# Two weight arrays begin 128 bytes later in SBUF, at multiples of 256 instead of odd multiples of 128

## The chip, the cores and the metric

The program runs on one core of a Trainium2 chip (8 cores, two dies). The metric is the device time in microseconds of one execution, the median of several. Lower is better. Five engines matter: TensorE (PE in the profile, with its weight loads as PEld), VectorE (DVE), ScalarE (ACT), GpSimd (POOL) and SyncE (SP), which issues the transfers of the weights.

## What is computed

Two kinds of transformer layer, two of each, run one after the other on one sequence of 512 tokens of width 1024 in float32. Cut to what matters here:

```python
for l in range(DEPTH):                       # DEPTH = 2, first kind
    h = rms_norm(x, norm_mix[l])
    z = h @ w_in[l]                          # then attention, a gated recurrence, a convolution
    x = x + mix @ w_out[l]
    h = rms_norm(x, norm_mlp[l])
    x = x + jnp.square(jax.nn.relu(h @ w_mlp_in[l])) @ w_mlp_out[l]
for l in range(DEPTH):                       # second kind: four mixers, gates, w_branch, w_out
    ...
    x = x + jnp.square(jax.nn.relu(h2 @ w_ff1)) @ w_ff2
```

Most of the work is in the products with weights: `w_in`, `w_out`, `w_branch` and the two matrices of each MLP.

## The kernel before

Everything is kept transposed in SBUF: 128 partitions hold features, 512 columns hold tokens. The weights come from memory as 518 units of 128 x 1024 float32 (512 KB), in the fixed order of the list `UNITS`; a layer of the first kind has 92 of them and one of the second kind 167. Each unit goes through the same steps:

- SP loads it into one of the two buffers of `w_raw` (`load_unit`, L255), as soon as the unit two before it has been split.
- ACT copies it to one of the three buffers of `w_hi` as fp32r, a float32 cut to the digits that one pass of TensorE takes (`split_hi`, L231), as soon as PE has finished the unit three before it.
- POOL computes the rest, `w_raw - w_hi`, into the same buffer of `w_lo` (`split_lo`, L278). For 36 units of the first two layers DVE does it (`split_lo_dve`, L247).
- PE multiplies: for each of 8 blocks of the inner dimension three matmuls add into one bank, high by high (L334), low weight by high activation (L335) and high weight by low activation (L336), in `Group.part`; `Group.some` has the same three at L306 to L308. The weight block is the stationary operand (128 x 128, 512 bytes of a partition), the activation the moving one (128 x 512). So the three matmuls of a block need three weight loads, from `w_hi`, `w_lo` and `w_hi`, and the whole program has 518 x 8 x 3 = 12,432 such pairs of load and matmul.

The activations are split in the same way by DVE: `hH` and `hL` for the input of a layer, `H2` and `L2` for that of an MLP, `midH` and `midL` for its hidden part. The other matmuls (attention, recurrence, sums) are plain float32 and don't touch the weight arrays.

The four engines work on the units in a ring, tied by semaphores; the order on each engine is written out by hand. DVE, ACT and POOL work beside PE. DVE's other work stands between the stages: norms (`pair`, L406), decays and gaps of the recurrences (L858, L2120), softmax (L749), the mixing of the branches (L2060).

SBUF is laid out by a stack: each call of `sb` puts a tensor behind the last one and fills it up to a multiple of `ALIGN` = 128 bytes. Four constants of 32 bytes each and a scratch of 2,048 bytes stand first, so the first tensor of the program, `xT`, begins at byte 2,176 of a partition, an odd multiple of 128. The sizes that follow are multiples of 256 up to the small tensors behind `yt`, except for `masks`; so `hH`, `hL`, `w_raw`, `w_hi`, `w_lo` and the constants `C` begin at odd multiples of 128 too, and `pair` and `yt` at multiples of 256. Of the tensors of the stages, those at multiples of 256 are, in the first two layers, `terms`, `probs`, `probsT`, `gap`, `QK` and a few more of the recurrence, and in the last two the compression weights `cw`. The others, `midH`, `midL`, `H2`, `L2`, `Z` and in the last two layers the counterparts of `probs`, `probsT`, `gap` and `QK` among them, are at odd multiples of 128. (The profile writes the counterparts under the same names, since it leaves numbers out.)

Of the kernel before, what the change touches and what calls it, by code (L numbers as in the profile page):

```python
# [19 lines left out]
U8 = mybir.dt.uint8  # L20
# [4 lines left out]
P = 128  # L25
# [16 lines left out]
ALIGN = 128  # L42
# [61 lines left out]
def program(nc, given, out):  # L104
# [5 lines left out]
    with ctx:  # L110
        used = {}

        def sb(name, shape, dt=F32, scope=ctx):


            used[name] = used.get(name, 0) + 1
            name = f"{name}_{used[name]}"
            tile = scope.enter_context(nc.sbuf_tensor(name, shape, dt))
            rest = (-(int(np.prod(shape[1:])) * BYTES[dt]) // 32 * 32) % ALIGN
            if rest:  # L120
                scope.enter_context(nc.sbuf_tensor(f"{name}_pad", [P, rest], U8))
            return tile
# [11 lines left out]
        hL = sb("hL", [P, NK, T], F32R)  # L134
        rstd = sb("rstd", [P, T])
        w_raw = sb("w_raw", [P, 2, UNIT])
        w_hi = sb("w_hi", [P, WB, UNIT], F32R)
        w_lo = sb("w_lo", [P, WB, UNIT], F32R)
        C = sb("C", [P, len(CONSTS), P])
        ident, ones, pair_ones, rot1, rot2, neg_tri, neg_ones = (C[:, i, :] for i in range(7))  # L140
        later_one = C[:, 10, :]
        Cb = sb("Cb", [P, 4, P], BF16)
# [107 lines left out]
        def load_unit(u):  # L250
            layer, j, _, nk, ntile, _ = UNITS[u]
            w = nk * ntile * P
            if u >= 2:
                wait_lo(sp, u - 2)
            sp.dma_start(w_raw[:, u % 2, 0:w], (w1_in if layer < DEPTH else w2_in)[layer % DEPTH, j, :, 0:w])\  # L255
                .then_inc(w_loaded[u % 2], 16)

        def load_vec(layer):
            n = NV1 if layer < DEPTH else NV2
            sp.dma_start(vecs[layer % 2][:, 0:n], (vec1_in if layer < DEPTH else vec2_in)[layer % DEPTH])\  # L260
                .then_inc(vec_loaded, 16)
# [701 lines left out]
        def load_start():  # L963

            scope = ExitStack()
            with scope:
# [4 lines left out]
                def on_sync():  # L971
                    sp.dma_start(C[:, 0, :], consts_in[:, 0, :]).then_inc(consts_loaded, 16)
                    load_vec(0)
                    load_unit(0)
                    for half in range(2):
                        c = slice(half * D // 2, half * D // 2 + D // 2)
                        sp.dma_start(x_tok[:, :, c], x_in[0, :, c].rearrange("(t p) d -> p t d", p=P))\
                            .then_inc(x_loaded[half], 16)
                    load_unit(1)
                    sp.dma_start(C[:, 1:, :], consts_in[:, 1:, :]).then_inc(matrices_loaded, 16)  # L980
                    sp.dma_start(masks_f[:, :, :], masks_in).then_inc(masks_loaded, 16)
                    sp.dma_start(pos[:, :], pos_in[0:1, :].to_broadcast([P, T])).then_inc(pos_loaded, 16)
                    sp.dma_start(freq[:, :], freq_in).then_inc(pos_loaded, 16)
                    sp.dma_start(cosT[:, :], rope_in[0]).then_inc(rope_loaded, 16)
                    sp.dma_start(sinT[:, :], rope_in[1]).then_inc(rope_loaded, 16)
# [26 lines left out]
                def on_vector():  # L1012
# [7 lines left out]
                    dve.wait_ge(matrices_loaded, 16)  # L1020
                    dve.tensor_copy(Cb[:, 0, :], C[:, 0, :])
                    dve.tensor_copy(Cb[:, 1:4, :], C[:, 7:10, :])
                    dve.wait_ge(pos_loaded, 32)
# [1289 lines left out]
```

## Time and profile before

| | |
|---|---|
| median of 3 runs | 3797.75 us (3796.26 to 3799.45) |
| profiled execution | 3801.36 us |
| its span, first to last instruction | 3800.0 us |
| mean granted TensorE clock | 0.977 |
| PE busy | 3653.7 us, 96% of the span |
| PEld busy | 2813.1 us, 74% |
| DVE busy | 2157.0 us, 57% |
| ACT busy | 1309.1 us, 34% |
| POOL busy | 1197.5 us, 32% |

The busy time of an engine counts each moment once, however many of its instructions overlap in it. Matmuls are pipelined: one begins before the last has ended, so the distance from one start to the next, and not the duration, is what a matmul costs in a dense stretch.

### The profile page before, as it was taken

The numbers are of one execution on the slowest core, as the hardware profiler recorded it, in microseconds if no ns is written. First come the engines' busy times: TensorE is split into PE (matmuls) and PEld (weight loads), VectorE is DVE, ScalarE is ACT, GpSimd is POOL, SyncE is SP. The second block draws the span as 40 slices with busy tenths as digits, with TensorE's granted clock in tenths as the row PEclk, the third lists the DMA queues.
The fourth block names the chain that finished last, engine by engine and source line by source line (L and its number), as shares of the span: only waits on it lengthen the run. The fifth ranks groups of instructions, "written<-read, shape, count | busy, mean of one in ns | idle before, by whom it ended". The sixth has DMA issues, their size and how long they took to land.

```text
span 3800.0 us, 44699 instructions
## 1 busy us (share of the span) xinstructions
PE 3653.7 (96%) x17876; PEld 2813.1 (74%) x17876; DVE 2157.0 (57%) x3048; ACT 1309.1 (34%) x2226; POOL 1197.5 (32%) x486
## 2 busy tenths in 40 slices
PE   8889999998899999999999999999999999999998
PEld 6646888865588888676777678887767777778887
DVE  7787565688754474633374485545553255365444
ACT  6344121443522131545423531122354433342112
POOL 0002444200144443132333244444213232334443
PEclk9889999997999999999999999999999999999999
DMA  4101333220033333121222132334112122223332
GB/s 134 44 12 50 98 97 95 93 69 12 23 95 99 95 120 105 40 67 56 78 62 77 51 93 96 95 99 147 51 34 79 61 78 62 67 73 95 97 97 83
DMA packets 80797, 292.38 MB, mean 77 GB/s; under 512 B 9648, under 2 KB 11088, under 8 KB 80080
## 3 DMA queue, kind: packets, MB, share of 16 engines
q1 hardware_dynamic: 77808, 278.49, 23.5%
q10 hardware_dynamic: 2784, 11.03, 0.9%
q8 instruction: 143, 2.34, 0.2%
q14 instruction: 62, 0.51, 0.0%
HBM read 285.30 MB, written 2.10 MB: 76 GB/s over the span
## 4 chain that ended last, share of the span: by engine, by line
PE 85%; DVE 11%; issue 2%; ACT 2%; DMA 0%; SPq 0%; DVEq 0%; ACTq 0%
PE acc L334 23%; PE acc L336 22%; PE acc L335 22%; PE banks L939 2%; PE banks L658 2%; PE banks L614 2%; DVE conv_c L1317 2%; PE banks L641 2%; PE banks L950 1%; DVE stat L738 1%; PE banks L1648 1%; DVE probs L749 1%; DVE QK L867 1%; DVE w_lo L247 1%; DVE pair L406 1%
## 5 line engine op out<-in xcount | busy, mean ns | idle before, releaser
L278 POOL TENSOR_TENSOR w_lo<-w_raw,w_hi 128x1024 fp32r<-128x1024 f32 x482 | 1197.3, 2484 | 2575.5 <-ACT w_hi L231 2575.5
L231 ACT ACTIVATE w_hi<-w_raw 128x1024 fp32r<-128x1024 f32 x518 | 548.9, 1060 | 1725.2 <-PE acc L336 1641.7
L334 PE MATMUL acc<-hH,w_hi 128*128 128x512 f32 x1776 | 732.3, 412 | 13.2 <-DVE sig L2036 6.6
L336 PE MATMUL acc<-hL,w_hi 128*128 128x512 f32 x1776 | 700.6, 395 | 0.0
L335 PE MATMUL acc<-hH,w_lo 128*128 128x512 f32 x1776 | 699.6, 394 | 0.0
L334 PEld LDWEIGHTS acc<-hH,w_hi 128*128 128x128 f32 x1776 | 338.5, 191 | 99.2 <-issue 25.0
L334 PE MATMUL acc<-H,w_hi 128*128 128x512 f32 x1024 | 400.5, 391 | 3.8 <-DVE L L398 3.8
L369 DVE TENSOR_TENSOR xT<-acc,xT 128x512 f32<-128x512 f32 x160 | 110.6, 691 | 517.0 <-PE acc L336 498.5
L334 PE MATMUL acc<-midH,w_hi 128*128 128x512 f32 x1024 | 401.0, 392 | 0.3
L335 PE MATMUL acc<-midH,w_lo 128*128 128x512 f32 x1024 | 398.8, 389 | 0.0
L336 PE MATMUL acc<-midL,w_hi 128*128 128x512 f32 x1024 | 398.7, 389 | 0.0
L336 PE MATMUL acc<-L,w_hi 128*128 128x512 f32 x1024 | 398.5, 389 | 0.0
L335 PE MATMUL acc<-H,w_lo 128*128 128x512 f32 x1024 | 398.5, 389 | 0.0
L336 PEld LDWEIGHTS acc<-hL,w_hi 128*128 128x128 f32 x1776 | 337.5, 190 | 73.7
L335 PEld LDWEIGHTS acc<-hH,w_lo 128*128 128x128 f32 x1776 | 338.9, 191 | 66.7 <-issue 4.3
L334 PEld LDWEIGHTS acc<-midH,w_hi 128*128 128x128 f32 x1024 | 192.2, 188 | 46.3 <-DVE midL L506 7.0
L334 PEld LDWEIGHTS acc<-H,w_hi 128*128 128x128 f32 x1024 | 192.2, 188 | 45.9 <-DVE L L398 5.5
L335 PEld LDWEIGHTS acc<-H,w_lo 128*128 128x128 f32 x1024 | 192.2, 188 | 40.6 <-issue 1.0
L336 PEld LDWEIGHTS acc<-midL,w_hi 128*128 128x128 f32 x1024 | 192.2, 188 | 40.2
L336 PEld LDWEIGHTS acc<-L,w_hi 128*128 128x128 f32 x1024 | 192.2, 188 | 40.0
L335 PEld LDWEIGHTS acc<-midH,w_lo 128*128 128x128 f32 x1024 | 192.3, 188 | 39.3
L505 DVE CAST midH<-relu 128x512 fp32r<-128x512 f32 x64 | 160.2, 2504 | 2.2
(332 smaller groups left out, 4716.7 us busy)
## 6 DMA issues: line engine op xcount, KB each, us to landing
w_raw<-in_stream SPq DMA_DIRECT2D x518, 512.0 KB, 3.6
cw<-in_cmpw ACTq DMA_DIRECT2D x2, 2048.0 KB, 7.3
mixed<-in_cmpw ACTq DMA_DIRECT2D x2, 2048.0 KB, 12.6
x_tok<-in_x SPq DMA_DIRECT2D x2, 1024.0 KB, 7.4
out<-probsT SPq DMA_DIRECT2D x4, 512.0 KB, 4.0
stack<-Z ACTq DMA_DIRECT2D x8, 128.0 KB, 2.2
stack<-Z ACTq DMA_DIRECT2D x8, 127.8 KB, 2.4
masks_f<-in_masks SPq DMA_DIRECT2D x1, 960.0 KB, 11.9
```

The costliest lines, as they stand in the source:

```text
L231: act.activation(w_hi[:, u % WB, 0:w], w_raw[:, u % 2, 0:w], ACT.Copy).then_inc(hi_split, 1)
L278: pool.tensor_tensor(w_lo[:, u % WB, 0:w], w_raw[:, u % 2, 0:w], w_hi[:, u % WB, 0:w], ALU.subtract)\
L334: pe.matmul(acc[n % 2][:, :], wh, H[:, k, :], start=(k == 0), stop=False)
L335: pe.matmul(acc[n % 2][:, :], wl, H[:, k, :], start=False, stop=False)
L336: last = pe.matmul(acc[n % 2][:, :], wh, Lo[:, k, :], start=False, stop=(k == nk - 1))
L369: dve.tensor_tensor(xT[:, i, :], a[:, :], xT[:, i, :], ALU.add).then_inc(up(free), 1)
L505: link(dve, dve.tensor_copy(midH[:, i, :], r))
L614: last = pe.matmul(self.score_banks[h % 3][:, 0:m], w["q"][r, qt * P:(qt + 1) * P], w["k"][r, lo * P:hi * P], start=True, stop=True, skip_ ...
L641: last = pe.transpose(self.turn_banks[n % 2][:, j * P:(j + 1) * P], self.P[:, s % 3, a, j * P:(j + 1) * P], ident)
L658: pe.matmul(self.out_bank[HD * a:HD * a + HD, cols], w["v"](kt, a), self.PT[:, a, kt, cols], start=(first and kt == 0), stop=True, skip_gr ...
L939: last = pe.matmul(scores, KK[r, jt * P:(jt + 1) * P], moving, start=(j == 0), stop=True, skip_group_check=True)
L1317: ins = dve.scalar_tensor_tensor(conv_c[:, j, :], src, vec[:, w:w + 1], conv_c[:, j, :], ALU.mult, ALU.add)
```

## The change

Two unused tensors of 128 bytes are put into the stack, one ahead of `w_hi` and one behind `w_lo`:

```diff
         w_raw = sb("w_raw", [P, 2, UNIT])
+        sb("ahead_of_halves", [P, ALIGN], U8)
         w_hi = sb("w_hi", [P, WB, UNIT], F32R)
         w_lo = sb("w_lo", [P, WB, UNIT], F32R)
+        sb("behind_halves", [P, ALIGN], U8)
         C = sb("C", [P, len(CONSTS), P])
```

Nobody writes or reads them. The addresses in a partition, from the two built programs:

| tensor | before | remainder by 256 | after | remainder by 256 |
|---|---|---|---|---|
| `w_raw` | 53,376 | 128 | 53,376 | 128 |
| `w_hi` | 61,568 | 128 | 61,696 | 0 |
| `w_lo` | 73,856 | 128 | 73,984 | 0 |
| `C` | 86,144 | 128 | 86,400 | 128 |
| all behind `C` | | | 256 higher | as before |

`xT`, `hH`, `hL` and `rstd` stand ahead of the arrays and don't move. Every engine issues the same instructions in the same order with the same semaphores; only addresses differ, and the line numbers behind the edit are two higher.

## Rows read from the trace of the kernel before

**Rows 1.** The page: busy time of each engine; then the clock in 40 slices.

```profile
PE 3653.7 (96%) x17876; PEld 2813.1 (74%) x17876; DVE 2157.0 (57%) x3048; ACT 1309.1 (34%) x2226; POOL 1197.5 (32%) x486
...
PEclk9889999997999999999999999999999999999999
```

**Rows 2.** Busy us by window in two MLPs: PE, PEld, DVE, ACT, POOL, clock.

```profile
540.00:640.00 100.00, 99.99 (x442) 82.48 (x441) 48.99 (x48) 20.17 (x19) 44.22 (x19) 1.00 0.32 99
2400.00:2500.00 100.00, 99.99 (x441) 82.49 (x440) 43.96 (x43) 19.94 (x19) 44.58 (x19) 1.00 0.32 97
```

**Rows 3.** The page, groups: count | busy us, mean ns | idle before.

```profile
L278 POOL TENSOR_TENSOR w_lo<-w_raw,w_hi 128x1024 fp32r<-128x1024 f32 x482 | 1197.3, 2484 | 2575.5 <-ACT w_hi L231 2575.5
L231 ACT ACTIVATE w_hi<-w_raw 128x1024 fp32r<-128x1024 f32 x518 | 548.9, 1060 | 1725.2 <-PE acc L336 1641.7
L334 PEld LDWEIGHTS acc<-hH,w_hi 128*128 128x128 f32 x1776 | 338.5, 191 | 99.2 <-issue 25.0
```

**Rows 4.** Timeline of an MLP of the first layer: start us, duration us.

```profile
620.04 0.39 PE L335 MATMUL acc<-midH,w_lo 128*128 128x512 f32 x1
...
622.11 1.06 ACT L231 ACTIVATE w_hi<-w_raw 128x1024 fp32r<-128x1024 f32 x1 [4.38 <-PE acc L336]
...
623.25 2.40 POOL L278 TENSOR_TENSOR w_lo<-w_raw,w_hi 128x1024 fp32r<-128x1024 f32 x1 [3.04 <-ACT w_hi L231]
...
625.48 0.39 PE L335 MATMUL acc<-midH,w_lo 128*128 128x512 f32 x1
```

**Rows 5.** Weight loads of L1648: duration ns min/median/max, first and last start.

```profile
L1648 PEld LDWEIGHTS banks<-cblocks,cw x128: 186/192/193, 1481.4 to 2676.6; 128*128 128x128 f32 x128
L1648 PEld LDWEIGHTS banks<-cblocks,mixed x128: 191/192/193, 1500.3 to 2695.5; 128*128 128x128 f32 x128
```

**Rows 6.** Timeline of L1648, PE alone: sixteen matmuls with each weight tensor.

```profile
1481.78 1.95 PE L1648 MATMUL banks<-cblocks,cw 128*128 128x62 f32 x16
...
1500.80 1.95 PE L1648 MATMUL banks<-cblocks,mixed 128*128 128x62 f32 x16
```

**Rows 7.** Line L641, first two layers and then the last two.

```profile
L641 PEld LDWEIGHTS banks<-C,probs x256: 137/141/232, 246.2 to 1005.0; 128*128 128x128 f32 x128
...
L641 PEld LDWEIGHTS banks<-C,probs x464: 137/140/146, 1538.0 to 3360.6; 128*128 128x128 f32 x155
```

**Rows 8.** Float32 matmuls with moving operand `pair`, and with `soft_sb`.

```profile
L413 PE MATMUL banks<-pair,C x16: 590/592/593, 27.7 to 3439.8; 128*128 128x512 f32 x16
...
L1722 PE MATMUL banks<-soft_sb,C x32: 589/592/697, 1721.4 to 3008.2; 128*128 128x512 f32 x32
```

**Rows 9.** Two groups of ACT by form.

```profile
L957 ACT ACTIVATE sp_part_sb<-sp_part_sb 128x512 f32<-128x512 f32 x32 | 20.2, 631 | 1.0
...
L957 ACT ACTIVATE terms<-terms 128x512 f32<-128x512 f32 x16 | 10.1, 633 | 0.5
```

**Rows 10.** Line L867 of DVE, first two layers and then the last two.

```profile
L867 DVE TENSOR_TENSOR QK<-Z,gap x72: 674/684/2254, 98.6 to 910.7; 128x512 f32<-128x512 f32 x72
...
L867 DVE TENSOR_TENSOR QK<-Z,gap x36: 677/684/694, 1913.8 to 3179.0; 128x512 f32<-128x512 f32 x36
```

**Rows 11.** Line L278, POOL's subtraction: durations.

```profile
L278 POOL TENSOR_TENSOR w_lo<-w_raw,w_hi x482: 2342/2404/2971, 6.6 to 3770.8; 128x1024 fp32r<-128x1024 f32 x161
```

**Rows 12.** Waits of PEld: who waited for POOL, us in total, times, longest.

```profile
PEld acc L334 <- POOL w_lo L278: 1.8, 3, 0.8
```

**Rows 13.** Timeline of a stage between the MLPs: POOL and DVE.

```profile
1898.76 2.39 POOL L278 TENSOR_TENSOR w_lo<-w_raw,w_hi 128x1024 fp32r<-128x1024 f32 x1 [4.29 <-ACT w_hi L231]
1898.83 3.41 DVE L2120 TENSOR_TENSOR_SCAN cum<-C,Z 128x512 f32<-128x512 f32 x1
```

**Rows 14.** Chain that ended last: start us, us, piece.

```profile
153.62 2.75 DVE Z L1364
...
1906.98 1.23 DVE cum L2120
...
3434.56 2.89 DVE pair L406
```

## The prediction

> **What bounds the kernel now.** I read the page first. PE is busy 96% of the span and its clock stands near full speed in nearly all slices [rows 1]; the other engines are busy 57% of the span at most. Then two windows of 100 us in the MLPs of the first and of the third layer: PE is never free there, at granted clock 1.00, and 442 and 441 matmuls touch each window, which is one every 227 ns [rows 2]. The timeline gives it more exactly: from a matmul of L335 that starts at 620.04 to one that starts at 625.48 there are 24 matmuls, 5.44 / 24 = 226.7 ns apart [rows 4]. Each of them has a weight load of its own; the load lasts 188 to 191 ns, but lies under the matmul before it [rows 3]. The 12,432 pairs at 226.7 ns make 2818 us, 74% of the span. So the time is PE's pace in this stream, and behind it the stages between the MLPs, where PE and DVE take turns on the chain [rows 14].
>
> Durations come from the profiled execution, 3801.36 us, with a span of 3800.0 us. The median of the runs is 3797.75 us, 3.6 us or 0.1% less, so differences are carried over to the median one for one.
>
> **What the change does, part by part.** It adds no instruction, wait or transfer, and moves none. The two new tensors are never touched. What is left are the instructions that read or write `w_hi` and `w_lo` at their new place. Everything behind the arrays keeps its remainder by 256, and `w_raw`, into which the transfers go, doesn't move at all, so no transfer of weights gets another start. What could differ for the tensors behind is only a remainder by 512 or more. `midH` is at remainder 384 by 512 in the first layer and at 128 in the third, and the two windows show the same pace [rows 2]: 0 for that.
>
> Term 1, the weight load. If loads from a multiple of 256 were quicker or slower, it would show where PE does little but load. Line L1648 is such a place: 62 columns move through each 128 x 128 block of weights. Its weights come once from `cw`, at a multiple of 256, and once from `mixed`, at an odd multiple of 128, with the same moving operand. The loads have the same median, 192 ns [rows 5], and sixteen matmuls take 1.95 us with either [rows 6]. Line L641 agrees: it loads `probs` from a multiple of 256 in the first two layers and from an odd multiple of 128 in the last two, at medians of 141 and 140 ns [rows 7], while its moving operand in `C` is at an odd multiple of 128 in both. So the case that the change makes, weights at a multiple of 256 against a moving operand at an odd multiple of 128, is in the trace already and costs nothing there. Likewise a moving operand at a multiple of 256 (`pair`) and at an odd multiple of 128 (`soft_sb`) against weights in `C` take 592 ns both [rows 8]. Cost: 0 x 12,432.
>
> The Trainium skill says of this (page "SBUF — State Buffer", section "SBUF: two separate sides" with its table of ports) that TensorE reads the moving operand and the weights through two ports of their own that wait for nobody; by that rule the place of the weights could not matter, and the rows above agree.
>
> What no row shows is the same pair of places in fp32r with 512 columns, since all such matmuls use the two arrays. I bound it. From below: 512 columns at 2.4 GHz are 213.3 ns, so at most 226.7 - 213.3 = 13.4 ns can go, 12,432 x 13.4 = 167 us. From above I take as much again, since the trace shows no collision to price: the load of 191 ns [rows 3] has 36 ns of room in 226.7. I take 0, the value of the nearest rows. Between lie steps of one tick of 2.4 GHz, 0.42 ns, or 5.2 us over the stream.
>
> Term 2, ACT's copy into `w_hi`, 1060 ns [rows 3]. ACT writes 512 elements in 631 ns at an odd multiple of 128 and in 633 ns at a multiple of 256 [rows 9], 2 ns apart. It is hidden too: in the MLP the copy ends at 623.17, POOL's subtraction at 625.65 [rows 4], and PE needs the unit only after two others, 2 x 5.44 us after it released the buffer near 622.1, at about 633. Cover 7 us; 0.
>
> Term 3, POOL's subtraction, which reads `w_hi` and writes `w_lo`: 482 times, median 2404 ns [rows 11]. Nearly nobody waits for its result, 1.8 us in all [rows 12], and POOL sits idle 2575.5 us [rows 3]. It costs time in another way. At 1898.83 DVE starts a scan and holds it for 3.41 us, over POOL's subtraction from 1898.76 to 1901.15, [rows 13], though the same scan of the next run takes 1.23 us on the chain [rows 14]. Going through the whole chain I find 31 pieces of DVE of more than 2 us of this kind, from 153.62 to 3434.56, of which the first and the last are shown [rows 14]. So each nanosecond of the subtraction may cost up to 31 ns of the chain. The trace has no subtraction on POOL at another place. DVE's product of two SBUF operands, L867, has a median of 684 ns with both `gap` and `QK` at multiples of 256 and with both at odd multiples of 128 [rows 10], and is the nearest row by kind. The ends are POOL's own spread [rows 11]: 62 ns less than the median gives 31 x 0.062 = 1.9 us, 567 ns more gives 31 x 0.567 = 17.6 us. I take 0.
>
> Term 4, DVE's 36 subtractions L247 on the same arrays: by the same row of L867, 0.
>
> Sum: 0 + 0 + 0 + 0, so 3797.75, rounded to 3798 us. A measurement of this kernel tells about 0.2% from no change, 7.6 us.
>
> **The rivals.** A, the stream gets faster (0.07). The 13.4 ns over the 213.3 could be the meeting of the two reads, since the weights and the moving operands now start at the same remainder by 256. If all of it went, the time would be 3798 - 167 = 3631 us; two ticks of 0.42 ns give 3788. Against it: rows 5 to 8 show no sign of the remainder.
>
> The Trainium skill (page "TensorE: Matmul & The Clock Gate", section "Wait — 56ns, not 53.3ns?") gives 215.7 ns from start to start for warm bf16 matmuls of 512 columns; this trace has 226.7 ns, and if placement explained the 11 ns between them, 12,432 x 11 = 137 us would go, an estimate of 3661 us. The page names no placement.
>
> B, slower by POOL (0.03). One mechanism: the subtraction takes longer at the new place, and each of the 31 DVE pieces on the chain that waits for it to end grows with it. At 10% (240 ns) it is 7.4 us, 3805 us, the point from which it decides; at 20%, 14.9 us and 3813 us. It needs no delay of PE by `w_lo` itself. C, slower by PE (0.03): the new remainder makes a meeting of reads where there was none. Two ticks give 10.4 us, 3808 us; the 13.4 ns of the upper bound give 3965 us. D, POOL gets 10% quicker (0.01): 3790 us.
>
> The change not doing what it says is no rival: the addresses are in the program, and the arrays are at their new places.
>
> **How the numbers follow.** The forecast of no effect has 0.86. Faster is A and D, 0.08; slower is B and C, 0.06. Within the forecast the median may move by what the three runs show, 3796.26 to 3799.45, some 1.6 us to each side, and by small changes in how DVE and POOL meet on the chain, which I allow 3 us more. With a tick of PE's pace to each side (5.2 us), which also takes in the lower end of POOL's bound, the range is 3791 to 3805 us. What lies outside is the body of the rivals, under 0.14.
>
> **What would show it.** In the profile after, the line of L278 keeps its median near 2404 ns, the weight loads of the stream theirs of 188 to 191 ns, ACT's copy 1060 ns, and 24 matmuls of the MLP take 5.44 us; the chain still has some 31 long pieces of DVE. A step of the pace would show as other than 441 or 442 matmuls in a window of 100 us: at 213.3 ns it would be 469. If POOL is the cause, the median of L278 moves and `pair` at L406 on the chain with it (2.89 us now). The prediction is wrong if fp32r streams care for a remainder that float32 matmuls don't care for, or if POOL does where DVE doesn't.

## The result, and the profile after

| | us | runs | range |
|---|---|---|---|
| before | 3798.18 | 4 | 3796.26 to 3799.45 |
| after | 3861.44 | 4 | 3859.35 to 3861.95 |

The ratio of the runs is 1.0163, with a 95% interval of 1.0151 to 1.0175. The kernel is slower by 63 us, and above the predicted range of 3791 to 3805 us. The profiled execution after took 3861.95 us, with a span of 3860.6 us, 60.6 us longer than before.

The page after, its first lines and its clock, as in [rows 1]:

```profile
span 3860.6 us, 44699 instructions
...
PE 3720.3 (96%) x17876; PEld 2818.8 (73%) x17876; DVE 2152.9 (56%) x3048; ACT 1309.6 (34%) x2226; POOL 1202.1 (31%) x486
...
PEclk9889999997999999999999999999999999999999
```

PE is still busy 96% of the time, so no new idle time has come in, and the clock is as it was. The same two windows in the MLPs as in [rows 2]. The columns are the stretch, its length, then busy time with the number of instructions for PE, PEld, DVE, ACT and POOL, PE's granted clock, DMA share and GB/s:

```profile
540.00:640.00 100.00, 100.00 (x431) 80.59 (x430) 43.62 (x42) 19.10 (x18) 43.85 (x18) 1.00 0.32 95
2400.00:2500.00 100.00, 100.00 (x431) 80.86 (x430) 50.87 (x48) 19.10 (x18) 43.48 (x18) 1.00 0.32 95
```

431 matmuls touch each window, where 442 and 441 did. The granted clock is 1.00 (the level of 2.4 GHz) in both, so the clock is not the reason. The timeline of PE at the place of [rows 4]: start us, us, instruction. L337 is the L335 of before.

```profile
620.10 0.39 PE L337 MATMUL acc<-midH,w_lo 128*128 128x512 f32 x1
...
625.70 0.39 PE L337 MATMUL acc<-midH,w_lo 128*128 128x512 f32 x1
```

24 matmuls lie between the two rows, 5.60 / 24 = 233.3 ns apart, where it was 226.7. The other lines that the prediction named, from the page's groups and from the answers on POOL's line, the waits and the chain:

```profile
L280 POOL TENSOR_TENSOR w_lo<-w_raw,w_hi 128x1024 fp32r<-128x1024 f32 x482 | 1201.9, 2494 | 2630.9 <-ACT w_hi L233 2630.9
L233 ACT ACTIVATE w_hi<-w_raw 128x1024 fp32r<-128x1024 f32 x518 | 548.7, 1060 | 1781.8 <-PE acc L338 1702.9
...
L336 PEld LDWEIGHTS acc<-hH,w_hi 128*128 128x128 f32 x1776 | 339.7, 191 | 104.8 <-issue 24.6
...
L280 POOL TENSOR_TENSOR w_lo<-w_raw,w_hi x482: 2340/2410/2973, 6.8 to 3830.8; 128x1024 fp32r<-128x1024 f32 x161
...
PEld acc L336 <- POOL w_lo L280: 1.5, 2, 0.8
...
3486.74 2.89 DVE pair L408
```

ACT's copy takes 1060 ns as before, the load shows 191 ns as before, POOL's subtraction a median of 2410 ns against 2404, and PEld waits 1.5 us for POOL, where it waited 1.8 [rows 3, 11, 12]. The last long piece of `pair` on the chain has the same 2.89 us as in [rows 14].

**Where the 60.6 us are.** I took from both traces the distance from the start of each matmul of the stream to the start of the next. Distances of 260 ns or more, which are pauses, count with the rest of the span. Worked out so:

| | distances | sum us | mean ns | rest of the span us |
|---|---|---|---|---|
| before | 11,723 | 2664.5 | 227.3 | 1135.5 |
| after | 11,710 | 2724.7 | 232.7 | 1135.9 |

The stream takes 60.2 us more and everything else 0.4 us more. After, 13 distances fewer (about 3 us) count with the stream and stand with the rest; all 12,432 matmuls of the stream have a record in both traces. That doesn't change the reading: the loss is PE's pace. It is even: with hH, midH, H2 and yH as the moving operand, in the first two layers and in the last two, the means are 232.6 to 232.9 ns. It does not depend on who else is at work: while POOL is busy the mean is 232.7 ns and while it is idle 232.7; for ACT it is 232.6 and 232.7, for DVE 232.6 and 232.8. Before, the distances in the stream are 226 and 227 ns one after the other. After, they go up and down between 228 and 241 ns in patterns that repeat, near 540 us for instance 230, 232, 228, 230, 233, 241, 232.

### The profile page after: what moved, and what is told of

It reads as the page before. It is cut to its first block, busy times and chain, and to the rows that moved or that the text cites. A ratio compares the mean times of both kernels' runs of the same rounds, so it can differ in the third digit from the quotient of the medians.

```text
span 3860.6 us, 44699 instructions
## 1 busy us (share of the span) xinstructions
PE 3720.3 (96%) x17876; PEld 2818.8 (73%) x17876; DVE 2152.9 (56%) x3048; ACT 1309.6 (34%) x2226; POOL 1202.1 (31%) x486
## 4 chain that ended last, share of the span: by engine, by line
PE 85%; DVE 11%; issue 2%; ACT 2%; DMA 0%; SPq 0%; DVEq 0%; ACTq 0%
PE acc L336 23%; PE acc L338 23%; PE acc L337 23%; PE banks L941 3%; PE banks L660 2%; PE banks L616 2%; DVE conv_c L1319 2%; PE banks L643 2%; PE banks L952 1%; DVE stat L740 1%; PE banks L1650 1%; DVE probs L751 1%; DVE QK L869 1%; DVE w_lo L249 1%; DVE pair L408 1%
## 5 line engine op out<-in xcount | busy, mean ns | idle before, releaser
L233 ACT ACTIVATE w_hi<-w_raw 128x1024 fp32r<-128x1024 f32 x518 | 548.7, 1060 | 1781.8 <-PE acc L338 1702.9
L336 PE MATMUL acc<-hH,w_hi 128*128 128x512 f32 x1776 | 740.9, 417 | 11.9 <-DVE sig L2038 6.2
L338 PE MATMUL acc<-hL,w_hi 128*128 128x512 f32 x1776 | 708.6, 399 | 0.0
L337 PE MATMUL acc<-hH,w_lo 128*128 128x512 f32 x1776 | 708.2, 399 | 0.0
L336 PEld LDWEIGHTS acc<-hH,w_hi 128*128 128x128 f32 x1776 | 339.7, 191 | 104.8 <-issue 24.6
L336 PE MATMUL acc<-H,w_hi 128*128 128x512 f32 x1024 | 406.2, 397 | 3.3 <-DVE L L400 3.3
L336 PE MATMUL acc<-midH,w_hi 128*128 128x512 f32 x1024 | 406.3, 397 | 0.0
L337 PE MATMUL acc<-H,w_lo 128*128 128x512 f32 x1024 | 404.2, 395 | 0.0
L337 PE MATMUL acc<-midH,w_lo 128*128 128x512 f32 x1024 | 404.1, 395 | 0.0
L337 PEld LDWEIGHTS acc<-hH,w_lo 128*128 128x128 f32 x1776 | 340.5, 192 | 73.3 <-issue 4.3
L336 PEld LDWEIGHTS acc<-H,w_hi 128*128 128x128 f32 x1024 | 192.7, 188 | 51.3 <-DVE L L400 5.0
L336 PEld LDWEIGHTS acc<-midH,w_hi 128*128 128x128 f32 x1024 | 192.7, 188 | 49.6 <-DVE midL L508 5.2
L337 PEld LDWEIGHTS acc<-H,w_lo 128*128 128x128 f32 x1024 | 192.7, 188 | 46.3 <-issue 1.0
L337 PEld LDWEIGHTS acc<-midH,w_lo 128*128 128x128 f32 x1024 | 192.7, 188 | 44.6
L507 DVE CAST midH<-relu_sb 128x512 fp32r<-128x512 f32 x64 | 160.6, 2509 | 2.2
```

Source lines behind the costliest of these rows:

```text
L233: act.activation(w_hi[:, u % WB, 0:w], w_raw[:, u % 2, 0:w], ACT.Copy).then_inc(hi_split, 1)
L336: pe.matmul(acc[n % 2][:, :], wh, H[:, k, :], start=(k == 0), stop=False)
L337: pe.matmul(acc[n % 2][:, :], wl, H[:, k, :], start=False, stop=False)
L338: last = pe.matmul(acc[n % 2][:, :], wh, Lo[:, k, :], start=False, stop=(k == nk - 1))
L507: link(dve, dve.tensor_copy(midH[:, i, :], r))
```

## The experiments

The theory that I formed: what counts is the place of the weights against the place of the moving operand, modulo 256 bytes. Before, both start at an odd multiple of 128, a difference of 0; after, the difference is 128. The rivals: the place of the weights by itself (loads from multiples of 256 are slow); the space between the tensors, and what moved by 128 between the two gaps; and contention with ACT and POOL, which write the two arrays. Below, "difference" is the start of the moving operand less that of the weights, modulo 256. The mean distances in the stream (pauses left out as above) come from the trace of each run. The three lines of the stream, L334 to L336 before, stand some lines lower in the kernels with more lines, up to L346.

**1. Weights or gap.** Four kernels; the edits are gaps that nothing touches.

```diff
+ sb("gap_0", [P, 256], U8)    # e1: ahead of w_hi
+ sb("gap_0", [P, 128], U8)    # e2: ahead of w_hi
+ sb("gap_1", [P, 128], U8)    # e2: ahead of w_lo
+ sb("gap_0", [P, 128], U8)    # e3: ahead of w_lo
+ sb("gap_1", [P, 128], U8)    # e3: ahead of C
+ sb("gap_0", [P, 128], U8)    # e4: ahead of xT, the first tensor
```

> Both weight arrays 256 bytes later, so they begin at odd multiples of 128 again, and everything behind them 256 bytes later, just as in the changed kernel. In the trace of the changed kernel a matmul of the stream starts every 232.7 ns instead of 226.8. Theory 1 (the remainder of the weights by 256 against that of the moving operand) and theory 2 (the remainder of the weights by itself): pace 226.8 ns, time 3798 us. Theory 3 (what costs is that the tensors behind the arrays have moved by 256, or the distance between w_raw and the arrays): pace near 232.7 ns, about 3861 us.

> Only w_hi at a multiple of 256, w_lo at an odd multiple of 128. w_hi is loaded for two of the three matmuls of a block. If each load pays for its own place (theories 1 and 2): 2/3 of the 63 us, 3840 us, with the pace lost only where w_hi is loaded. If what counts is that w_hi and w_lo are alike (theory 4: successive loads from different remainders): as slow as or slower than 3861 us or, if unlike is good, below 3798 us.

> Only w_lo at a multiple of 256. Theories 1 and 2: one load of three pays, 3798 + 21 = 3819 us, and e2 and e3 together make the 63 us. Theory 4 (alike or unlike) gives the same time for e2 and e3.

> 128 bytes ahead of xT: weights, hH, hL, H2, L2, midH, midL all begin at multiples of 256, their remainders relative to one another are those of the kernel before. Theory 1 (relative): pace 226.8 ns, 3798 us. Theory 2 (the weights' own remainder): pace 232.7 ns, about 3861 us.

| | moved by 128 | time us | ratio, 95% interval | mean ns after hi x H, lo x H, hi x L, in the MLPs |
|---|---|---|---|---|
| e1 | nothing (256) | 3797.84 | 0.9998, 0.9988 to 1.0007 | 226.8 to 226.9 |
| e2 | `w_hi` alone | 3864.73 | 1.0173, 1.0157 to 1.0188 | 232.8, 234.8, 232.2 |
| e3 | `w_lo` alone | 3838.47 | 1.0109, 1.0092 to 1.0126 | 232.5, 234.1, 226.7 |
| e4 | everything | 3799.59 | 1.0001, 0.9992 to 1.0010 | 226.7 to 226.9 |

The windows of e1, e3 and e4, columns as above:

```profile
2400.00:2500.00 100.00, 99.98 (x441) 82.47 (x440) 43.57 (x42) 19.52 (x19) 45.00 (x19) 1.00 0.31 96
```

```profile
2400.00:2500.00 100.00, 100.00 (x433) 81.36 (x432) 46.21 (x44) 19.11 (x18) 43.63 (x19) 1.00 0.31 95
```

```profile
2400.00:2500.00 100.00, 99.99 (x442) 82.46 (x441) 43.63 (x43) 19.11 (x19) 43.72 (x18) 1.00 0.31 98
```

441 matmuls in e1 and 442 in e4, as before, 433 in e3. e2 and e3 did not come out as expected (3840 and 3819 us): they lose 65 and 39 us beside the runs of before that were taken with them, 104 together and not 63. So it is not that each load pays a price of its own, which adds up. e1 moves the weights, and all that lies behind them, by 256, and loses nothing: neither the gap nor the remainder by 512 matters. e4 puts the weights at multiples of 256, exactly as the change does, but the activations too, and loses nothing: the place of the weights by itself does not matter either. What is left is the difference between the two.

**2. The activations instead of the weights.** e8 leaves the remainder of the weights by 256 as it was and moves all high and low activations by 128. The two gaps around `hH` and `hL` stand ahead of the weights and move `w_raw`, `w_hi` and `w_lo` by 256 bytes, which e1 showed to cost nothing.

```diff
  xT = sb("xT", [P, NK, T])
+ gap_of(128)
  hH = sb("hH", [P, NK, T], F32R)
  hL = sb("hL", [P, NK, T], F32R)
+ gap_of(128)
...  # the same around midH and L2, midH2 and midL2, yH and yL, H2_2 and L2_2
```

> All activations of the stream at multiples of 256, weights where they were before. Theory 1 (relative): the same difference of 128 as in the changed kernel, 3861 us and 232.7 ns. Theory 2: 3798 us and 226.8 ns.

It took 3865.36 us, ratio 1.0172 (1.0156 to 1.0187), with means of 232.3 to 232.7 ns. The window of e8:

```profile
2400.00:2500.00 100.00, 100.00 (x431) 80.90 (x430) 50.85 (x49) 19.10 (x18) 43.46 (x19) 1.00 0.31 95
```

431 matmuls, as after the change, although `w_raw`, `w_hi` and `w_lo`, all that ACT and POOL read and write for the weights, have kept their remainder by 256. With e4 this settles the cause as far as places go: it is relative.

**3. Half of the activations.** In e6 only the low halves are moved, in e7 only the high ones. The gaps are those of e8, around each low or each high array.

```diff
+ gap_of(128)    # e6: ahead of hL and behind it; e7: ahead of hH and behind it
...  # the same around the halves of mid, H2, y and H2_2
```

> Only the low halves of the activations (hL, L2, midL, yL) at multiples of 256; they move through PE in the third matmul of a block, L336. Theory 1a: a weight load is held up by the matmul that it lies under, when the two read from different remainders; then one load of three is held, the distance after the third matmul and the one after the first of the next block grow to 232 to 234 ns and the one after the second stays 227; time like e3_lo_only, 3838 us. Theory 1b: a matmul is slow when its own weights and its moving operand differ; then the distances after the second and the third matmul grow and the one after the first stays 227; also near 3838 us. Theory 2: 3798 us.

> Only the high halves of the activations (hH, H2, midH, yH) at multiples of 256, which move in the first two matmuls of a block. Theories 1a and 1b: two loads or matmuls of three differ, like e2_hi_only, 3865 us. Theory 2 (the weights' own remainder): 3798 us.

e6 took 3856.23 us, ratio 1.0152 (1.0137 to 1.0168); e7 took 3821.50 us, ratio 1.0059 (1.0042 to 1.0075). Expected were 3838 and 3865 us, so this is the wrong way round for a simple count. In e6 one matmul in three (hi x L) has a difference of 128, in e7 two in three (hi x H and lo x H). Yet in the last two layers with `H2` e6 shows 230.0, 235.8 and 234.2 ns, 20 ns more per three matmuls than 3 x 226.7, and e7 228.4, 232.5 and 225.9 ns, 7 ns more. In the first two layers e6 shows 227.0, 229.0 and 234.3 there. The numbers of the first two layers are means over two paces. The timeline of e6 in one MLP, around a short pause, with `midH` and `midL`:

```profile
591.36 0.39 PE L340 MATMUL acc<-midH,w_hi 128*128 128x512 f32 x1
...
593.42 0.39 PE L340 MATMUL acc<-midH,w_hi 128*128 128x512 f32 x1
...
595.93 0.40 PE L342 MATMUL acc<-midL,w_hi 128*128 128x512 f32 x1
596.30 0.50 PE L340 MATMUL acc<-midH,w_hi 128*128 128x512 f32 x1
596.64 0.39 PE L341 MATMUL acc<-midH,w_lo 128*128 128x512 f32 x1
...
597.10 0.39 PE L340 MATMUL acc<-midH,w_hi 128*128 128x512 f32 x1
...
599.20 0.39 PE L340 MATMUL acc<-midH,w_hi 128*128 128x512 f32 x1
```

Ahead of the pause nine matmuls in 2.06 us are 228.9 ns each, behind it nine in 2.10 us are 233.3 ns. `H2` of the same layer has the quick pace from 377 to 414 us, over more than six units and so over all three buffers of the weights, and the slow one from 636 to 680 us. The same tensors at the same places thus have two paces, each of which repeats (226, 227, 234 ns, and 230, 236, 234 ns after hi x H, lo x H and hi x L) until a pause. In the MLPs of the last two layers nearly all blocks have the slow one. The price is not a fixed sum for each matmul.

**4. Which read meets which.** While PE streams the columns of one matmul, PEld loads the weights of the next. The expectations call one form of the theory 1a: the load meets the moving operand of the matmul that it lies under. The other is 1b: what counts is a matmul's moving operand against its own weights. e12 tells them apart. Its order is hi x H, hi x L, lo x H, with `w_lo` and the low activations at multiples of 256. Then every load lies under a matmul with the same remainder, but two matmuls of three differ from their own weights. e13 has the new order alone.

```diff
  pe.matmul(acc[n % 2][:, :], wh, H[:, k, :], start=(k == 0), stop=False)
- pe.matmul(acc[n % 2][:, :], wl, H[:, k, :], start=False, stop=False)
- last = pe.matmul(acc[n % 2][:, :], wh, Lo[:, k, :], start=False, stop=(k == nk - 1))
+ pe.matmul(acc[n % 2][:, :], wh, Lo[:, k, :], start=False, stop=False)
+ last = pe.matmul(acc[n % 2][:, :], wl, H[:, k, :], start=False, stop=(k == nk - 1))
...
+ gap_of(128)    # e12: ahead of w_lo and behind it, and around each low activation
```

> The second and third matmul of a block exchanged: high by high, high weight by low activation, low weight by high activation. All arrays at odd multiples of 128 as before. All theories: 226.8 ns and 3798 us; it is the base for e12.

> The same order, with w_lo and the low halves of the activations at multiples of 256 and the high halves at odd multiples of 128. Now each weight load lies under a stream that begins at the load's own remainder (high weights under high activation, low weights under low activation, high weights under high activation), while two of three matmuls have weights and moving operand at different remainders. Theory 1a (a load is held up by the stream that it lies under): 226.8 ns and 3798 us, no loss at all. Theory 1b (a matmul's own two operands): two of three matmuls slow, 231 to 233 ns, 3840 to 3865 us.

e13 took 3799.21 us, ratio 0.9998 (0.9988 to 1.0009). e12 took 3839.34 us, ratio 1.0107 (1.0090 to 1.0124), with a mean distance of 231.2 ns. The window of e12:

```profile
2400.00:2500.00 100.00, 100.00 (x432) 80.73 (x431) 46.06 (x44) 19.11 (x18) 43.79 (x19) 1.00 0.32 95
```

432 matmuls. So 1a falls as the whole cause: no load has another remainder than the operand it lies under, and 39 us are lost. 1b fits in size (two thirds of 63 us would be 42), but even the distance after hi x H, where the matmul's own operands are alike too, has grown, to 230.9 ns in the MLPs, and it does not fit the others: two of three differ in e7 and in e2 too, and 23 and 65 us are lost; one of three differs in e3 and in e6, and 39 and 57 us are lost. In e3 the distance after hi x H has grown too (232.5 ns), whose own operands are alike but under which `w_lo` is loaded from another remainder. Neither form holds alone.

**5. Other differences.** In e5 and e11 each pair of activations has a difference of its own, so that one run shows several. In e11 all activations but `hH` and `hL`, which have a gap, are slices that begin 1 to 60 elements inside a larger tensor.

```diff
+ gap_of(64)     # e5: ahead of hH; 192 behind hL; others ahead of and behind mid, H2, y
...
+ def sb_at(name, n, off, scope=ctx):    # e11
+     t = sb(name, [P, n * T + 64], F32R, scope)
+     return t[:, off:off + n * T].rearrange("p (k t) -> p k t", t=T)
```

> Weights stay at odd multiples of 128; the activations move by amounts that differ by stage. Activation minus weights by 256: hH and hL 64, midH and midL 192 in the first two layers and 224 in the last two, H2 and L2 32 and 96, yH and yL 128. If only the remainder by 128 of the difference counts in the sense of two banks of 128 bytes, 32 to 96 (partly in the other bank) lie between 226.7 and 232.7 ns and 128 is the worst; if every difference but 0 is as bad, all stages are near 232.7. yH at 128 is the control: weights where they were and activation moved, 232.7 ns by theory 1, 226.8 by theory 2 (weights' own remainder). The whole time is read only beside that.

> Activation minus weights by 256, by stage: hH and hL 160; H2 and L2 16 in the first two layers and 8 in the last two; midH and midL 4 and 240; yH and yL 48. e5_map had 229 ns at 64 and 232.5 to 233.4 ns at 32, 96, 128, 192 and 224. If the loss comes as soon as the two differ at all, every stage here is at 229 to 234 ns; if it needs a difference of some tens of bytes, 4, 8 and 16 stay at 226.8 ns. A stage below 226.7 ns would show a place that is better than that of the kernel before.

e5 took 3848.79 us, ratio 1.0131 (1.0110 to 1.0151), and e11 3876.86 us in its one run, beside 3798.04 us for the kernel before. The mean distances, with those of the runs above:

| difference, bytes | mean ns | run and operand |
|---|---|---|
| 0 | 226.7 | before, e4 |
| 4 | 236.6 | e11, mid, first layers |
| 8 | 233.4 | e11, H2, last layers |
| 16 | 231.7 | e11, H2, first layers |
| 32 | 233.3 | e5, H2, first layers |
| 48 | 232.0 | e11, y |
| 64 | 229.3 | e5, hH |
| 96 | 233.4 | e5, H2, last layers |
| 128 | 232.5 to 232.9 | after; e5, y |
| 160 | 234.1 | e11, hH |
| 192 | 233.3 | e5, mid, first layers |
| 224 | 233.3 | e5, mid, last layers |
| 240 | 235.4 | e11, mid, last layers |

The timeline of e11 in `midH` (difference 4):

```profile
619.87 0.40 PE L346 MATMUL acc<-midL,w_hi 128*128 128x512 f32 x1
...
625.55 0.40 PE L346 MATMUL acc<-midL,w_hi 128*128 128x512 f32 x1
```

and of e5 in `hH` (difference 64):

```profile
760.00 0.39 PE L342 MATMUL acc<-hL,w_hi 128*128 128x512 f32 x1
...
765.50 0.39 PE L342 MATMUL acc<-hL,w_hi 128*128 128x512 f32 x1
```

24 matmuls lie between each pair of rows: 5.68 / 24 = 236.7 ns and 5.50 / 24 = 229.2 ns. Of thirteen differences 0 is the best, 64 the next, and one of 4 bytes is the worst. It is no matter of even and odd multiples of 128 alone. The order of the others is weaker: most stand for one stage of one run, the stages have slightly different means at difference 0 too (226.7 ns for H2, 226.9 for mid, 227.9 for hH, 227.2 for y), and e6 has shown paces 4.4 ns apart at one and the same difference.

**6. Why the rows of before said nothing.** The prediction argued from matmuls of 62 and 128 columns. e9 and e10 take 512, 256, 128 and 384 columns in the MLPs and projections of layers 1 to 4, so the other columns of the tokens are left out of the computation; e10 also has the gaps of the change.

```diff
+ COLS = (512, 256, 128, 384)
...
+ m = COLS[UNITS[u][0]]
...
- pe.matmul(acc[n % 2][:, :], wh, H[:, k, :], start=(k == 0), stop=False)
+ pe.matmul(acc[n % 2][:, 0:m], wh, H[:, k, 0:m], start=(k == 0), stop=False)
...
+ gap_of(128)    # e10: ahead of w_hi, and behind w_lo
```

> The kernel before with shorter streams: 512 columns of the activation move in the first layer as before, 256 in the second, 128 in the third, 384 in the fourth, so 3/4 to 1/4 of the tokens are left out of the products from the second layer on. Weights and activations at the same remainder by 256. Shows the pace by columns: 226.7 ns at 512 and, if the extra over the columns (13.4 ns at 2.4 GHz) is a cost of each matmul, about 173 at 384 and 120 at 256; at 128 the load binds, near the 112 ns of L1648.

> The same shorter streams with the weight arrays at multiples of 256, as in the changed kernel. Theory 1 with a fixed cost for each load: 6 ns more than e9_cols_same at 512, 384 and 256. With a cost for each column: 6, 4.5 and 3 ns. At 128 columns, where the load binds: no difference, as the rows of L1648 and L641 had none, which would show why these rows misled; a difference of 6 ns there would mean that float32 and fp32r behave differently.

e9 took 3451.65 us and e10 3479.65 us, in one run each. Their mean granted clock was 0.846 and 0.845, where the kernel before has 0.977, and it was 0.50 (the level of 1.2 GHz) in the MLP of the third layer of both. The windows there, with 128 columns, first of e9 and then of e10:

```profile
2100.00:2140.00 40.00, 39.74 (x187) 39.56 (x187) 19.71 (x19) 7.42 (x7) 19.14 (x8) 0.50 0.33 95
```

```profile
2100.00:2140.00 40.00, 40.00 (x187) 39.48 (x186) 34.82 (x31) 9.57 (x10) 19.57 (x8) 0.50 0.29 92
```

187 matmuls in either, one every 213 ns, so with 128 columns there is no loss at that level either. The mean distances at granted clock 1.00:

| columns | e9, difference 0 | e10, difference 128 |
|---|---|---|
| 512 | 227.0 | 232.5 |
| 384 | 173.7 | 175.8 |
| 256 | 119.7 | 118.9 |
| 128 | 111.7 | 111.7 |

The timelines of e9 with 384, 256 and 128 columns:

```profile
2434.99 0.33 PE L341 MATMUL acc<-hH,w_hi 128*128 128x384 f32 x1
...
2439.15 0.33 PE L341 MATMUL acc<-hH,w_hi 128*128 128x384 f32 x1
...
1223.65 0.28 PE L343 MATMUL acc<-midL,w_hi 128*128 128x256 f32 x1
...
1229.40 0.28 PE L343 MATMUL acc<-midL,w_hi 128*128 128x256 f32 x1
...
1543.52 0.27 PE L342 MATMUL acc<-hH,w_lo 128*128 128x128 f32 x1
...
1548.89 0.27 PE L342 MATMUL acc<-hH,w_lo 128*128 128x128 f32 x1
```

and those of e10:

```profile
2660.99 0.34 PE L343 MATMUL acc<-hH,w_hi 128*128 128x384 f32 x1
...
2665.21 0.34 PE L343 MATMUL acc<-hH,w_hi 128*128 128x384 f32 x1
...
1227.47 0.28 PE L345 MATMUL acc<-midL,w_hi 128*128 128x256 f32 x1
...
1233.17 0.28 PE L345 MATMUL acc<-midL,w_hi 128*128 128x256 f32 x1
...
1563.94 0.28 PE L344 MATMUL acc<-hH,w_lo 128*128 128x128 f32 x1
...
1569.30 0.28 PE L344 MATMUL acc<-hH,w_lo 128*128 128x128 f32 x1
```

With 384 columns 24 matmuls lie between the rows, 4.16 / 24 = 173.3 ns against 4.22 / 24 = 175.8. With 256 and with 128 there are 48: 5.75 / 48 = 119.8 against 5.70 / 48 = 118.8, and 5.37 / 48 = 111.9 against 5.36 / 48 = 111.7. The other remainder costs 5.5 ns with 512 columns, 2.1 with 384 and nothing with 256 or 128. A row of matmuls with 62 or 128 columns could not have shown it.

## Why the prediction was wrong, point by point

**Term 1 failed, and it alone.** The step was: "So the case that the change makes, weights at a multiple of 256 against a moving operand at an odd multiple of 128, is in the trace already and costs nothing there", and from it "Cost: 0 x 12,432". The rows were read rightly, and they have not changed: after, the loads of L1648 and L641 of before still have medians of 192 and 140 ns. But they carry 62 and 128 columns, and e10 shows that a difference of 128 is free in the stream too when the matmuls are that short. At 512 columns the term measures 232.7 - 227.3 = 5.4 ns; times the 11,710 distances that is 63 us, less 3 us for the 13 distances fewer (13 x 227 ns): the 60.2 us of the accounting. The lines of `C` [rows 8] do have 512 columns, but they are float32, and slower: the 592 ns are durations, and two in a row take 0.86 us on the chain after the change, 430 ns each, nearly twice what a matmul of the stream takes.

```profile
3491.72 0.86 PE banks L415 x2
```

I did not measure whether the meeting is hidden there or does not exist for float32.

The text named this weak place itself ("What no row shows is the same pair of places in fp32r with 512 columns") and put it down to "fp32r streams". e9 and e10 show the length to matter, within fp32r. Whether fp32r matters besides stays open. The term's bound from above, 13.4 ns, did hold the 5.4 ns, but the chance that it was given, 0.03 for rival C, was far too small: with the bound at 167 us and no row of the same kind, the nearest rows deserved less trust.

**The rule on the ports.** With 512 columns every run with a difference other than 0 shows PE's pace to depend on where its two operands lie against each other: 226.7 ns at 0, up to 236.6 at 4 bytes. The Trainium skill (page "SBUF — State Buffer", section "SBUF: two separate sides") was read in the prediction as saying that the place of the weights cannot matter. By that reading e8, after and e11 would all have kept 226.7 ns; the measurement decides, and the reading falls for matmuls of 384 and 512 columns. At 256 and 128 columns no run speaks against it; only the difference 128 was tried there.

**Rival C was the case** as far as shown: PE slower by the new remainder. That the reads meet, as it says ("the new remainder makes a meeting of reads where there was none"), is argued. It was sized at two ticks, 3808 us, and at most at 3965; the mean was 5.4 ns or 13 ticks, 3861 us. Rival A, that the reads met before and would be freed, had the sign wrong: 0 is the one difference without a loss. As for the 13.4 ns above the columns' own time, they remain at 512, 384 and 256 columns with difference 0: 226.7 - 213.3 = 13.4, 173.3 - 160.0 = 13.3, 119.8 - 106.7 = 13.1 (the columns at 2.4 GHz). So they don't grow with the columns, as the loss by the difference does. What they are is not shown.

**Terms 2, 3 and 4 and the tensors behind held.** ACT 1060 ns and 1060; POOL 2404 and 2410 ns, which by the 31 pieces would be 0.2 us; the long DVE pieces of the chain are the same in number and sum (33 of over 1.3 us in each trace, 87.1 and 87.2 us). Rivals B and D therefore did not occur. The tensors behind cost nothing, as e1 shows.

**What the prediction's signs told.** It asked for 24 matmuls in 5.44 us, and for 441 or 442 per window. Both showed the fault at once: 5.60 us and 431. The loads' 188 to 191 ns did not: the load shows 191 ns still.

**What stays open.** Shown is that the loss is in the stream's pace, that it follows the difference of the places modulo 256, and that at a difference of 128 it is there with 384 and 512 columns and not with 256. Not shown is which read holds up which, or that a meeting of reads is the cause at all. 1a alone is refuted by e12. 1b does not add up between e6, e7 and e12. The repeating patterns, and the two paces of e6 for the same instructions, suggest that the phase between a load and the stream settles into one of several steady forms. That is argued, not shown, and the records of the loads don't show it: in both paces of e6 a load starts 2 to 4 ns behind the start of a matmul and takes 187 or 188 ns. Pauses differ from kernel to kernel, so such kernels can't be sized better than some ns per matmul from the map above.

## What to carry to other kernels

In a dense stream of fp32r matmuls of 512 columns, give the weights and the moving operands starts that are equal modulo 256 bytes, all of them, high and low halves alike, and check it after each edit that allocates something ahead of one of them: it is worth 5.4 ns in 227 per matmul here, and up to 10. When a price is looked up in other rows of a trace, take rows that are bound by the same thing. A matmul bound by its weight load says nothing of one that is bound by its columns. Take the same length too: with 256 columns, where the columns also set the pace, the difference cost nothing (118.9 against 119.7 ns).

## What the runs showed of the hardware

- A shift of 4 bytes between the operands costs more (236.6 ns, one run) than one of 128 (232.7 ns) or of 64 (229.3 ns).
- The pace of load and matmul in fp32r at granted clock 1.00 is the columns' time at 2.4 GHz plus 13.1 to 13.4 ns at 512, 384 and 256 columns, and 111.7 ns at 128. Float32 matmuls of 62 columns (L1648) have 112 ns too, so the columns don't set that one; that the load does is argued.
- At granted clock 0.50 the distances are 427, 320 and 213 ns at 512, 384 and 256 columns (e9), the columns' time at 1.2 GHz and nothing on top, and 213 ns at 128 too.
- At 256 columns the other remainder was even a little quicker, 118.9 ns against 119.7. One run of each does not settle it.
- Matmuls on the same tensors at the same places can run in two steady paces, 228.9 and 233.3 ns, and change from one to the other at a pause (e6).
